# Output product, layer norms, routing and experts with tokens on the partitions: a one-hot scatter one pair later, an fp32 gather, 16 weight slots

## What is computed

```
mix = merged @ w_out
x = layer_norm(ALPHA * x + mix, ln1_g, ln1_b)              # over 1024 features
aff = softmax(x @ w_router)                                # 512 tokens, 16 experts
gate, idx = top_k(aff.T, 64)                               # each expert takes 64 tokens
h = x[idx] @ w_gate_up[e]                                  # 64 x 1024 times 1024 x 2048
ye = (silu(h_gate) * h_up) @ w_down[e] * gate              # 64 x 1024 times 1024 x 1024
ffn = zeros.at[idx].add(ye)
x = layer_norm(ALPHA * x + ffn, ln2_g, ln2_b)
```

## Time and profile before

| | us |
|---|---|
| three runs, median | 2297.7 (2294.46 to 2298.14) |
| profiled execution, its own time | 2297.08 |
| profiled execution, span of its instructions | 2295.3 |
| TensorE busy | 2132.7 (93%) |
| VectorE (DVE) busy | 1102.7 (48%) |
| ScalarE (ACT) busy | 715.8 (31%) |
| GpSimd (POOL) busy | 182.7 (8%) |

### The profile page before, as it was taken

One profiled execution on the slowest core, in us unless ns is written; L12 is line 12 of the kernel. 1 busy time (PEld: TensorE's weight loads), 2 busy tenths in 40 slices (PEclk: granted clock), 3 DMA queues, 4 the chain that ended last, 5 costly groups with the idle time before them and its releaser, 6 DMA issues.

```text
span 2295.3 us, 24304 instructions
## 1 busy us (share of the span) xinstructions
PE 2132.7 (93%) x9854; PEld 1506.7 (66%) x9854; DVE 1102.7 (48%) x1540; ACT 715.8 (31%) x1035; POOL 182.7 (8%) x175
## 2 busy tenths in 40 slices
PE   5989999999999999999999999999995999999995
PEld 4768888888777778888878666777872333333331
DVE  6886443445656564434466575554546111111114
ACT  2554322223455443223333454333323000000002
POOL 2221000001000010000010100431012000000001
PEclk9999999999999999999999999999996999999997
DMA  4222323324121222232233211332315999999991
GB/s 165 83 74 92 101 75 118 101 69 121 68 68 59 66 93 86 83 116 99 74 122 106 53 60 60 70 81 69 101 46 238 382 378 402 417 404 413 406 417 76
DMA packets 83663, 350.75 MB, mean 153 GB/s; under 512 B 9152, under 2 KB 10832, under 8 KB 66912
## 3 DMA queue, kind: packets, MB, share of 16 engines
q1 hardware_dynamic: 80448, 342.92, 40.8%
q0 software_dynamic: 2240, 2.71, 0.9%
q10 hardware_dynamic: 864, 3.57, 0.4%
HBM read 347.06 MB, written 2.10 MB: 152 GB/s over the span
## 4 chain that ended last, share of the span: by engine, by line
PE 82%; DVE 10%; ACT 4%; issue 3%; POOL 0%; DMA 0%; ACTq 0%; DVEq 0%; POOLq 0%
PE PS L1674 19%; PE PS L1676 18%; PE PS L1675 18%; PE PS L1982 10%; PE PS L2013 5%; PE PS L2025 2%; PE PS L1965 2%; PE PS L1717 2%; PE PS L1779 1%; DVE XC L1322 1%; PE PS L1793 1%; PE PS L1803 1%; DVE X L1565 1%; PE PS L1860 1%; DVE WL L1256 1%
## 5 line engine op out<-in xcount | busy, mean ns | idle before, releaser
L1674 PE MATMUL PS<-HH,WH 128*128 128x512 f32 x1392 | 561.7, 403 | 35.3 <-DVE HL L1260 21.7
L1675 PE MATMUL PS<-HL,WH 128*128 128x512 f32 x1392 | 547.7, 393 | 0.0
L1676 PE MATMUL PS<-HH,WL 128*128 128x512 f32 x1392 | 547.5, 393 | 0.0
L1256 DVE TENSOR_TENSOR WL<-RAW,WH 128x1024 fp32r<-128x1024 f32 (+5 forms) x300 | 341.9, 1140 | 251.3 <-ACT WH L1001 249.6
L1001 ACT ACTIVATE WH<-RAW 128x1024 fp32r<-128x1024 f32 (+4 forms) x278 | 263.2, 948 | 311.1 <-PE PS L1676 311.0
L1674 PEld LDWEIGHTS PS<-HH,WH 128*128 128x128 f32 x1392 | 264.4, 190 | 112.4 <-issue 31.3
L1676 PEld LDWEIGHTS PS<-HH,WL 128*128 128x128 f32 x1392 | 264.6, 190 | 56.9
L1675 PEld LDWEIGHTS PS<-HL,WH 128*128 128x128 f32 x1392 | 265.2, 190 | 54.9 <-issue 2.0
L1982 PE MATMUL PS<-SL,XS 128*64 128x512 f32 x952 | 227.2, 596 | 0.0
L1363 DVE TENSOR_TENSOR X<-X,PS 128x512 f32<-128x512 f32 x116 | 79.6, 686 | 228.6 <-PE PS L2025 162.4
L1982 PEld LDWEIGHTS PS<-SL,XS 128*64 128x64 f32 x952 | 70.1, 137 | 133.8 <-issue 126.8
(11 more groups left out here) (292 smaller groups left out, 2661.7 us busy)
## 6 DMA issues: line engine op xcount, KB each, us to landing
SL<-in_wgu_dram SPq DMA_DIRECT2D x119, 1024.0 KB, 11.6
SL<-in_wdn_dram SPq DMA_DIRECT2D x60, 1024.0 KB, 9.4
RAW<-in_w_dram SPq DMA_DIRECT2D x46, 512.0 KB, 3.3
RAW<-in_wg_dram SPq DMA_DIRECT2D x44, 512.0 KB, 3.2
RAW<-in_wu_dram SPq DMA_DIRECT2D x44, 512.0 KB, 3.3
RAW<-in_wd_dram SPq DMA_DIRECT2D x32, 384.0 KB, 3.1
RAW<-in_wqkv_dram SPq DMA_DIRECT2D x24, 512.0 KB, 3.3
RAW<-in_wd_dram SPq DMA_DIRECT2D x32, 320.0 KB, 2.9
```

Of the source, the lines that this page charges most:

```text
L1256: e.tensor_tensor(wl, raw, wh.bitcast(F), ALU.subtract).then_inc(*wlo.did("u", u))
L1674: e.matmul(out, wh[:, w], xh, start=k == 0, stop=False)
L1675: e.matmul(out, wh[:, w], xl, start=False, stop=False)
L1676: m = e.matmul(out, wl[:, w], xh, start=False, stop=k == g.total - 1)
```

## The change

- **Output product.** The contraction index is the outer loop; tokens are on the partitions, and eight PSUM banks (4 token blocks x 2 halves) accumulate all 192 products. The residual enters them first, as X times identity in fp32. The factor 0.5 moves into GH and GL. A weight unit is now a slice across all output chunks, in runs of 512 bytes.
- **Layer norms** per block of 128 tokens: bn_stats, bn_aggr, a root on ACT, reciprocal and shift on DVE, normalisation by ACT from PSUM into XF. Gain and offset of the first norm are folded: into the router weights (and a bias LB, made in `m2_consts` by a new product that waits for a DVE product), into the copy after the gather, and into `alpha_x`.
- **Routing.** XF is turned into X, half by ACT, half by DVE; logits have tokens on the partitions. Eight rounds of match_replace mark the chosen with -1, and there is no tie logic.
- **Gather** in fp32 from XF: four products a chunk in place of eight.
- **Scatter.** The one-hot is turned without gates; the gates of the slots come from 16 products with one column (`slot_gates`) and scale the result as it is split into YOH and YOL. Scatter of pair i - 1 stands behind `up` of pair i, two fp32r products per block and half. In pair 7 the sum is carried in PSUM by identity products, and the second norm reads it there. At the end XF is turned back block by block, and ACT and DVE apply gain and offset.
- **Weight slots.** 16 in place of 14. Loads 0 to 3 wait for the last product of the last branch, 4 and 5 for the last GL, 6 to 15 for the end of the output product.
- RS, ST, SQ and SA are given up after the dense part, and ACC and YP change places in memory.

```diff
+NSLOT = 16
 NGATE = 4
...
-    for c in range(DC):
-        o.lin(("w2o", c), [("w2o", (c,), 8)], "g", fresh=c == 0)
...
+    for tb in range(4):
+        for h in range(2):
+            o.claim("mix", tb, h)
+    o.add("residual")
+    for k in range(DC):
+        u = o.unit("w2o", (slice(None), slice(None), k), 8)
+        o.add("split", u + AHEAD)
+        o.add("mix", k, u)
+
+
+def layer_norm_order(o, n, source, signal, then):
+    def norm(tb):
+        o.add("norm", n, tb)
+        for h in range(2):
+            o.release((source, tb, h), "lnx", "x", n, tb, h)
+        then(tb)
+
+    for tb in range(4):
+        o.add("stat", n, tb)
+        if tb:
+            norm(tb - 1)
+    norm(3)
...
+    def turned(tb):
+        for h in range(2):
+            o.claim("xt", tb, h)
+        o.add("x_turn", tb)
+        o.release(("xt", tb, 0), "xnat", tb)
+        o.release(("xt", tb, 1), "route", "xt", tb)
+        if tb == 0:
+            o.claim("lg")
+        else:
+            o.add("logits", tb - 1)
+
+    layer_norm_order(o, 0, "mix", "lin", turned)
+    o.add("logits", 3)
+    o.add("affinity")
...
+    def scatter(i):
+        for tb in range(4):
+            for h in range(2):
+                o.claim("sc", i, tb, h)
+                o.add("scatter", i, tb, h)
+                o.release(("sc", i, tb, h), "xup", "sc", i, tb, h)
...
         if i == 0:
             o.add("alpha_x")
+        else:
+            scatter(i - 1)
+        if i % 2 == 0:
+            o.claim("gw", q)
+            o.add("slot_gates", q)
+            o.release(("gw", q), "xs", "gw", q)
+            for j in range(2):
+                o.claim("gt", "e", q, j)
+                o.add("scatter_t", q, j)
+                o.release(("gt", "e", q, j), "turn", "gt", q, j)
...
+            if i == 7 and k < 3:
+                for h in range(2):
+                    o.claim("fin", k, h)
+                o.add("carry", k)
...
+            o.release(("y", i, n), "lo", "y2", i, n)
+    for tb in range(4):
+        if tb == 3:
+            for h in range(2):
+                o.claim("fin", tb, h)
+            o.add("carry", tb)
+        for h in range(2):
+            o.add("scatter", 7, tb, h)
...
-            e.wait_ge(*xup("w2o", DC - 1))
             for i, (src, two) in enumerate(loads):
                 j = i % NSLOT
+                if i == 0:
+                    e.wait_ge(*lin(*o.last(("br", 0, DC - 1))))
+                elif i == 4:
+                    e.wait_ge(*lo("g", DC - 1))
+                elif i == 6:
+                    e.wait_ge(*lin("mix", 3))
                 if i >= NSLOT:
                     e.wait_ge(*ex("w", (i - NSLOT) // 2))
                 dst = SL[j][:, :].rearrange("p (a n) -> p a n", a=2) if two else SL[j][:, :]
                 e.dma_start(dst, src).then_inc(*d_slot[j].did(i))
...
+                    e.activation(GH[:, d, :], ACC[:, d, :], ACT.Copy, scale=0.5).then_inc(*hi.did("g", d))
...
+                        e.activation(XF[:, tb, 512 * h:512 * h + 512], bank(("mix", "fin")[n], tb, h), ACT.Identity,
+                                     bias=SD[:, 2, tb:tb + 1], scale=SD[:, 1, tb:tb + 1]).then_inc(
+                            *lnx.did("x", n, tb, h))
...
+                    e.activation(rows(tb, 0), bank("xt", tb, 0).rearrange("p (c t) -> p c t", c=4), ACT.Copy).then_inc(
+                        *xnat.did(tb))
...
+                    e.activation(YOH[:, 512 * n:512 * n + 512], bank("y", i, n), ACT.Copy, scale=GA[:, i:i + 1]).then_inc(
+                        *hi.did("y2", i, n))
...
+                        e.tensor_tensor(W, WRT[:, :, :],
+                                        V[:, VEC[name]:VEC[name] + DC].unsqueeze(2).to_broadcast([128, DC, NE]),
+                                        ALU.mult).then_inc(*scaled.did("router", n))
...
+                elif kind == "stat":
+                    n, tb = a
+                    e.wait_ge(*(lin("mix", tb) if n == 0 else ex("sc", 7, tb, 1)))
+                    for h in range(2):
+                        e.bn_stats(BN[:, tb, h, :], bank(("mix", "fin")[n], tb, h)).then_inc(*ln.did("stat", n, tb, h))
+                    e.wait_ge(*ln("stat", n, tb, 1))
+                    e.bn_aggr(MV[:, tb, :], BN[:, tb, :, :]).then_inc(*ln.did("var", n, tb))
+                elif kind == "norm":
+                    n, tb = a
+                    r = SD[:, 1, tb:tb + 1]
+                    e.wait_ge(*lnx("sd", n, tb))
+                    e.reciprocal(r, SD[:, 0, tb:tb + 1]).then_inc(*ln.did("rs", n, tb))
+                    e.wait_ge(*ln("rs", n, tb))
+                    e.tensor_scalar(SD[:, 2, tb:tb + 1], MV[:, tb, 0:1], r, -1.0, ALU.mult, ALU.mult).then_inc(
+                        *ln.did("shift", n, tb))
+                elif kind == "x_turn":
+                    tb, = a
+                    e.wait_ge(*tr("xt", tb, 1))
+                    e.tensor_copy(rows(tb, 1), bank("xt", tb, 1).rearrange("p (c t) -> p c t", c=4)).then_inc(
+                        *route.did("xt", tb))
...
+                        e.match_replace(out=WK[:, :], in_to_replace=T8[:, :], in_values=WK[:, :],
+                                        imm_value=-1.0).then_inc(*route.did("out", i))
+                    e.wait_ge(*route("out", CAP // 8 - 1))
+                    e.tensor_scalar(M1[:, :], WK[:, :], 0.0, None, ALU.is_lt).then_inc(*route.did("chosen"))
                     e.wait_ge(*route("chosen"))
-                    e.tensor_tensor_scan(M3[:, :], ON[:, :], M1[:, :], 0.0, ALU.mult, ALU.add).then_inc(*route.did("count"))
+                    e.tensor_tensor_scan(M3[:, :], ones[0:16, 0:1].to_broadcast([16, T]), M1[:, :], 0.0, ALU.mult,
+                                         ALU.add).then_inc(*route.did("count"))
...
+                    e.tensor_scalar(XS[q % 2][:, d, :], bank("ga", q, d)[:, 0:256], vec("l1g", d), vec("l1b", d), ALU.mult,
+                                    ALU.add).then_inc(*xs.did(q, d))
...
+                    e.wait_ge(*ex("gw", q))
+                    e.tensor_copy(GA[:, 2 * q:2 * q + 2], bank("gw", q)[:, 0:2]).then_inc(*xs.did("gw", q))
...
+                    else:
+                        e.tensor_tensor(y, y, new, ALU.add).then_inc(*xup.did("sc", i, tb, h))
...
+                    e.scalar_tensor_tensor(out=YOL[:, 512 * n:512 * n + 512], in0=bank("y", i, n), scalar=GA[:, i:i + 1],
+                                           in1=YOH[:, 512 * n:512 * n + 512].bitcast(F), op0=ALU.mult,
+                                           op1=ALU.subtract).then_inc(*lo.did("y2", i, n))
...
+                            e.wait_ge(*scaled("router", 0))
+                            for c in range(DC):
+                                m = e.matmul(bank("mask2")[:, 256:272], ones, QM[:, 0, 16 * c:16 * c + 16], start=c == 0,
+                                             stop=c == DC - 1)
+                        m.then_inc(*red.did("mask", n))
...
+                        for h in range(2):
+                            if o.before["mix", tb, h]:
+                                e.wait_ge(*freed("mix", tb, h))
+                            for c in range(4):
+                                e.matmul(bank("mix", tb, h)[:, 128 * c:128 * c + 128], rows(tb, h)[:, c, :], ident,
+                                         start=c == 0, stop=False, skip_group_check=True)
...
+                    for tb in range(4):
+                        xh, xl = (G[:, k, 128 * tb:128 * tb + 128] for G in (GH, GL))
+                        for h in range(2):
+                            out, cols = bank("mix", tb, h), slice(512 * h, 512 * h + 512)
+                            e.matmul(out, xh, wh[:, cols], start=False, stop=False, skip_group_check=True)
+                            e.matmul(out, xh, wl[:, cols], start=False, stop=False, skip_group_check=True)
+                            m = e.matmul(out, xl, wh[:, cols], start=False, stop=k == DC - 1, skip_group_check=True)
...
+                        e.wait_ge(*lnx("x", 0, tb, h))
+                        pe_turn(e, ("xt", tb, h), [XF[:, tb, 512 * h + 128 * c:512 * h + 128 * c + 128] for c in range(4)])
...
+                    for c in range(DC):
+                        m = e.matmul(bank("lg")[:, 16 * tb:16 * tb + 16], X[:, c, 128 * tb:128 * tb + 128], WRT[:, c, :],
+                                     start=c == 0, stop=c == DC - 1, skip_group_check=True)
...
-                        if q == 0:
-                            e.wait_ge(*xnl(3, 1))
-                    for tc in range(4):
-                        for P in (XNH, XNL):
-                            m = e.matmul(bank("ga", q, d)[:, 0:256], P[:, tc, 128 * d:128 * d + 128], PE[:, tc, :],
-                                         start=tc == 0 and P is XNH, stop=tc == 3 and P is XNL)
+                    for tb in range(4):
+                        m = e.matmul(bank("ga", q, d)[:, 0:256], XF[:, tb, 128 * d:128 * d + 128], PE[:, tb, :],
```

(89 more changed lines are left out.)

355 lines of the change are left out of this document (158 added, 197 removed).

## The result

Median 2284.0 us (2282.93 to 2285.79, four runs) against 2297.0 us for the kernel before (2294.46 to 2298.14, four runs): ratio 0.9946, 95% interval 0.9929 to 0.9963. On another chip, five runs beside the experiments gave 2284.0 again (0.994, 0.9928 to 0.9952). The change saves 13 us, less than half of the 28.7 forecast. The profiled execution took 2282.9 (span 2281.1).

| | before | forecast | after |
|---|---|---|---|
| TensorE reaches the output product | 1671.7 | 1676.1 | 1676.9 |
| output product ends | 1716.7 | 1728.6 | 1729.0 |
| logits end | 1746.7 | 1749.6 | 1752.5 |
| first gather | 1770.9 | 1770.0 | 1772.9 |
| last down product ends | 2255.7 | 2247 | 2258.4 |

The account below looks back on a forecast made before the run. The expert pairs were taken as TensorE's alone, with the weight stream nearly side by side. Pairs end at 2247, plus tail 19.9, 1.8 outside the span and 0.6 to the median: 2269 us, range 2252 to 2288.

Parts of the forecast that it names:

- steps 4 and 5: Expert pairs: fp32 gather at 1.75 a chunk, scatter behind the next up; 472.8 us against 484.8, plus 4 of load waiting.
- Step 1: Constants of mixer two: the new bias product waits ahead of the memory query, all 4.4 us later (bounds 0 and 6).
- Step 3: First norm, transposes, logits, routing: logits end +21 us behind the output product (bounds +16 and +35), first gather at 1770.0.
- a turn: First norm, per token block: DVE's small passes, ACT, transposes, copy and next statistics in sequence, 4.9 us.
- odd pairs: Expert pairs 3 and 5, with gathers but without slot gates and one-hot: 65.6 us each.
- even pairs: Expert pairs 2, 4 and 6, with slot gates and turned one-hot: 50.6 us each.
- early loads: Four to six expert loads beside the output product: costed at nothing, since what counts is when slots first come free.
- rival B: In-order turn on DVE: copies wait longer, turn 9 us, logits end at +35, time 2283; chance 0.15.
- slot gates: Even pairs, before the scatter: 32 passes over one column, 2.5 us (1.5 to 5).
- Step 6: Tail: last scatter, statistics, norm, transposes, one scaled copy, out transfer 2.1; 19.9 us for 39.6.
- rival A: Leaner TensorE, stream binds: first release at 1771, pairs end about 2232, time 2254; chance 0.12.
- C: Expert pairs: DVE additions not hidden, 5.5 us a pair, 38 if exposed seven times, time 2307; chance 0.06.
- D: Weight stream drops: loads over 2.66 us in the mean and the gain is gone; chance 0.02.

Follow-up runs that it names:

- turn: Changed kernel with the first layer norm's turns two blocks behind the statistics, not one: 2279.6 us, ratio 0.9917.
- turn2: Repeat of the changed kernel with the first layer norm's turns two blocks behind the statistics: 2279.8 us.
- turn_xroute: Changed kernel with turns two blocks behind the statistics and x turned during the routing, without the bias edit: 2272.0 us, ratio 0.988.
- the kernel with all four edits: Changed kernel with own bias bank, turns two blocks behind, x turned during routing, pair 6's scatter and two carries inside last up: 2253.2 us, repeated 2255.7.
- bias_turn: Changed kernel with the bias product in its own bank and step, and turns two blocks behind the statistics: 2266.2 us, ratio 0.9862.

## Why the prediction was wrong in size

**The direction and most of the mechanism held; the saving was 13 us and not 28.7.** The terms that failed are the pairs (steps 4 and 5: 472.8 and 4 of waiting forecast, 485.4 measured), the tail (19.9 and 22.7), and the clock in steps 1 and 3. Near their terms were: residual 7.1 (7.5), a turn 5.2 (4.9), first three gather chunks 8.1 (7.8), odd pairs 68.5 (65.6), even pairs 49.1 (50.6), early loads worth nothing, no scatter between down and up, waits for loads only in the last pair. The deferral of the scatter, forecast to keep TensorE fed, is worth 16.5 us by itself, the buffers 6.

**Step 1 was mis-sized: 4.4, measured 6.3 to 8.0.** The wait and the 16 passes were right (4.2 together). Left out was the clock: the query behind them ran at half. The profile's 1676.9 hides it, since that execution was 1.3 us ahead of the one before at the masks. The bound of 6 was too low.

**Step 3 had the logits warm.** Forecast +21 from the product's end, measured +23.5: two blocks at half clock, 6.65 us and not 4.0. This is the clock half of rival B, not its DVE half: the turn was not 9. That the time fell on B's 2283 is chance.

**Steps 4 and 5 carry most, 8.5 us: half is TensorE's own work, half the stream.** TensorE's own sum came to 485.4 - 8.5 = 476.9 against 472.8. A gather chunk took 1.92, not 1.75: 29 chunks are 4.9 us, the first three 0.3. Behind the wait for the one-hot the first chunk of pairs 1 and 5 ran in part at half clock and took 3.5 and 3.4. In pair 3 the clock fell only 1.2 us into the chunk (granted 1.00 up to 1966, then 0.50), which took 2.6, and the first `up` step behind it took 4.57 in place of 3.58. That is 4.7 in all. The carries took 0.95 each, not 0.85: 0.6. The slot gates gave 4 x 1.5 = 6.0 back (1.03, not 2.5). That is +4.5, within 0.5 of the sum. The rest is the stream: 8.5 us lost to it where 4 were booked. First free buffer 3.2 later (1784.6), 2.52 us a load and not 2.5 (3.5 over 176), 17.7 idle and not 15: 9.4 of the 10.7 us by which the last landing was late (2249.3 in place of 2238.6); for the other 1.3 I have no row. And the forecast let the last pair's scatter and carries stand behind its last wait without asking what they would cost there; moved ahead of it they gave 4.3.

**Step 6: 22.7, forecast 19.9. The term that failed is the output.** Behind the last turns come four scaled copies on VectorE (2272.8 to 2275.8), 3.0 us where the forecast had one of 0.7, and behind the last copy 5.3 us of output transfer where it had 2.1. The two are one limit: the eight pieces are 2.1 MB, and the DMA engines moved them without a pause at some 380 GB/s from 2274.2 to 2280.0. With two engines copying, the copies are done in 3 us and the transfer sets the end; before, eight copies of 0.67 in a row kept pace with it. By these rows I would expect fewer copies on VectorE to save little, and an earlier first piece to help; no run tried it. These two terms are 5.5 over. The statistics gave 1.8 back (6.4, not 8.2: the blocks step by 1.7, not 2.05), the last norm 0.6, and the hand-overs were less than the 0.5 booked.

Three sums of the prediction are slightly off as written, which changes nothing above: its pairs add up to 473.0 and not 472.8, its turn to 4.8 and not 4.9, and rival A's terms to 2252.4 and not 2254.

**The rivals.** A was right in what binds the last pair (half the bytes: -8.6) and wrong in where, since the first buffer came free at 1784.6, not 1771. C did not happen: DVE's additions held TensorE for 1.1 us in all. D did not: the stream ran at 416 GB/s. The Trainium skill (DMA: Bandwidth & Descriptors, Where 436 GB/s comes from) has the HBM side bind at about 358 GB/s per core, which would be 2.93 us a load (an estimate from the page); the trace of this one core at work again does not agree, with 2.52.

## What to carry to other kernels

In this kernel TensorE's chain and the weight stream ran side by side within 7 us of each other, and what an edit was worth hung on its place. Price such an edit by its place:

- Ahead of the first buffer that comes free, or where the stream stands on full buffers, it counts in full (turns 4.4, first scatter 7.4).
- Behind that, where the stream runs, only what exceeds the distance between the chains counts (7 us of products left out gained nothing; some 24 us added cost 16.5).
- Behind the last wait it counts in full again (4.3).

Before adding a step into a full queue, look for an engine's idle stretch that is already there: the same transposes cost 7 us in the first scatter and nothing during the routing. Price what follows a new wait, not only the wait. And when two engines share the last copies, ask whether the output transfer keeps pace (in the tail it didn't).

## What the runs showed of the hardware that was not expected

A wait of 2.25 us and 16 products over 16 columns on TensorE were followed by products at half clock for 3 to 5 us (0.43 for 0.23 us). A wait of 1.0 us was followed by a fall in turn, turn2, turn_xroute and one execution of the kernel with all four edits, and by none in another and in bias_turn. Each wait of 3.5 us ahead of a gather was followed by half clock for part of its first chunk, in pair 3 only after 1.2 us of it at full clock. With the scatter in its own pair, waits of 2.2 us and less (the longest) were followed by half clock in two downs and two scatters. Output of 2.1 MB in eight pieces moved at some 380 GB/s, the weights at 416. A bn_stats of 128x512 from PSUM took 0.68 us in the mean, two in a row 1.2 to 1.3. A copy of 128x256 from PSUM with gain and offset from two columns took 0.544 us, 0.12 more than the plain one before (0.424). The fp32 gather's passes over 256 columns stepped by 1.92/8 = 0.24, more than half of a pass over 512 (0.445).
